# Modulation products of a two-block transformer kernel: from TensorE to VectorE, with their weights outside the ring

## What is computed

```python
sc_x = jax.nn.silu(c)
sc_c = jax.nn.silu(c_ctx)
for l in range(DEPTH):
    mx = (sc_x @ ada_w[l] + ada_b[l]).reshape(bsz, 6, 1, d)
    mc = (sc_c @ ada_w[l] + ada_b[l]).reshape(6, d)
    hx = modulate(rmsnorm_2(x, norm_g[l, 0]), mx[:, 0], mx[:, 1])
```

## Time and profile before

| | |
|---|---|
| median of 3 runs | 4306.5 us (4297.13 to 4309.94) |
| the profiled execution: its own time, its span | 4302.7 us, 4300.9 us |
| mean granted clock of TensorE | 0.955 of full |
| TensorE (PE) matmuls, busy | 3941.1 us, 92% |
| TensorE weight loads (PEld) | 3224.4 us, 75% |
| VectorE (DVE) | 1837.2 us, 43% |
| ScalarE (ACT) | 1383.9 us, 32% |
| GpSimd (POOL) | 1422.2 us, 33% |

### The profile page before, as it was taken

One profiled execution on the slowest core, in us unless ns is written; L12 is line 12 of the kernel. 1 busy time (PEld: TensorE's weight loads), 2 busy tenths in 40 slices (PEclk: granted clock), 3 DMA queues, 4 the chain that ended last, 5 costly groups with the idle time before them and its releaser, 6 DMA issues. The chain is left out here.

```text
span 4300.9 us, 48720 instructions
## 1 busy us (share of the span) xinstructions
PE 3941.1 (92%) x19562; PEld 3224.4 (75%) x19562; DVE 1837.2 (43%) x3076; ACT 1383.9 (32%) x2082; POOL 1422.2 (33%) x644
## 2 busy tenths in 40 slices
PE   6999998999989999899997888899999879999998
PEld 4777766777777776777765777789999668876886
DVE  4544445644554444374354556331111555543113
ACT  3223334332332333432233444231111334443222
POOL 1225543655422453355550110122222100023442
PEclk9999999999999999999998998899999889999999
DMA  2123332444321233234431000112221100012332
GB/s 86 56 61 103 110 91 66 127 127 129 103 61 57 88 116 92 75 118 132 127 109 34 25 25 20 40 44 59 64 64 56 51 15 15 14 50 69 94 97 74
DMA packets 544397, 316.69 MB, mean 74 GB/s; under 512 B 35828, under 2 KB 517167, under 8 KB 544175
## 3 DMA queue, kind: packets, MB, share of 16 engines
q1 hardware_dynamic: 543903, 312.53, 24.6%
q10 hardware_dynamic: 272, 1.05, 0.1%
HBM read 311.44 MB, written 2.10 MB: 73 GB/s over the span
## 5 line engine op out<-in xcount | busy, mean ns | idle before, releaser
L443 POOL TENSOR_TENSOR wlo<-wraw,whi 128x1024 fp32r<-128x1024 f32 (+5 forms) x640 | 1422.0, 2228 | 2843.6 <-ACT whi L436 2842.3
L459 PE MATMUL acc<-hh,whi 128*128 128x512 f32 (+2 forms) x2744 | 1071.7, 391 | 71.0 <-POOL wlo L443 32.8
L461 PE MATMUL acc<-hh,wlo 128*128 128x512 f32 (+2 forms) x2744 | 1040.0, 379 | 0.0
L460 PE MATMUL acc<-hl,whi 128*128 128x512 f32 (+2 forms) x2744 | 1038.2, 378 | 0.0
L436 ACT ACTIVATE whi<-wraw 128x1024 fp32r<-128x1024 f32 (+5 forms) x640 | 625.9, 980 | 866.2 <-DMA wraw<-in_ffn_w 263.4
L459 PEld LDWEIGHTS acc<-hh,whi 128*128 128x128 f32 x2744 | 522.4, 190 | 212.7 <-POOL wlo L443 54.8
L460 PEld LDWEIGHTS acc<-hl,whi 128*128 128x128 f32 x2744 | 523.0, 191 | 91.0 <-issue 11.8
L461 PEld LDWEIGHTS acc<-hh,wlo 128*128 128x128 f32 x2744 | 522.1, 190 | 85.8
L1358 DVE TENSOR_TENSOR t<-acc,sq 128x768 f32<-128x768 f32 (+1 forms) x44 | 36.3, 825 | 501.6 <-PE acc L461 501.6
L459 PE MATMUL ob<-hh,whi 128*128 128x512 f32 (+2 forms) x576 | 219.9, 382 | 20.6 <-DVEq L764 20.1
L660 DVE TENSOR_SCALAR y<-acc 128x512 f32<-128x512 f32 (+1 forms) x80 | 59.6, 745 | 356.4 <-PE acc L461 356.4
(11 more groups left out here) (367 smaller groups left out, 6043.4 us busy)
## 6 DMA issues: line engine op xcount, KB each, us to landing
wraw<-in_ffn_w SPq DMA_DIRECT2D x120, 512.0 KB, 3.7
wraw<-in_w_in SPq DMA_DIRECT2D x102, 512.0 KB, 3.7
wraw<-in_ada_w SPq DMA_DIRECT2D x96, 512.0 KB, 3.9
wraw<-in_w_up SPq DMA_DIRECT2D x88, 512.0 KB, 3.9
wraw<-in_w_down SPq DMA_DIRECT2D x32, 512.0 KB, 4.3
wraw<-in_w_out SPq DMA_DIRECT2D x16, 512.0 KB, 4.1
wraw<-in_w_mkv SPq DMA_DIRECT2D x16, 512.0 KB, 4.0
wraw<-in_ab_w_in SPq DMA_DIRECT2D x14, 512.0 KB, 3.7
```

Source lines behind the costliest of these rows:

```text
L443: e.tensor_tensor(wlo[0:rows, s, a:b, 0:w], wraw[0:rows, s, a:b, 0:w], whi[0:rows, s, a:b, 0:w].bitcast(F32), ALU.subtract).then_inc(lo_re ...
L459: e.matmul(o, wh, xh, start=first, stop=False)
L460: e.matmul(o, wh, xl, start=False, stop=False)
L461: return e.matmul(o, wl, xh, start=False, stop=last)
```

## The change

The modulation slabs leave the ring. A buffer `ada_w` of its own takes one slab (2 x 512 numbers in each of 128 partitions), in the place where `row_f` was, and SyncE loads it straight behind a slab of the ring, when VectorE has used the one before (`ada_used`). ScalarE, GpSimd and TensorE do nothing with it. VectorE multiplies each of its two rows of tiles by the condition of that row, a number per partition, and adds to two running sums (128 x 512 for each of the two conditions), `ada_s` and columns 512 to 767 of `sq`. In the gates it does so behind its reads of gates 0 and 2, in the FFN's up part behind the convolution, between the reads of a pair, in the down part behind a read. The sum over the partitions is left to `pe_ada_out`, now eight f32 matmuls with 128 rows of weights and one column of ones, run behind the first slab of a pair or behind gate 0.

```diff
-        row_f = nc.alloc_sbuf_tensor_at("row_f", [4, AW2], F32, offset=229344 - 4 * AW2)
+        ada_w = nc.alloc_sbuf_tensor_at("ada_w", [P, 2, AW2], F32, offset=229344 - 4 * 3 * AW2)
+        ada_s = nc.alloc_sbuf_tensor_at("ada_s", [P, AW2], F32, offset=229344 - 4 * AW2)
...
         def load(e, c, parts, width=P, cols=None):
...
+            if ada_due and ada_due[0] == n:
+                ada_due.pop(0)
+                load_ada(e, c)
+
+        def load_ada(e, c):
+            n = c.count("ada")
+            l, u, part = n // (4 * ADA), n // 4 % ADA, n % 4
+            w = A["ada_w_2"][bass.ds(l, 1), part * 256:part * 256 + 256, bass.ds(u * AW2, AW2)]
+            if n % (4 * ADA) == 0:
+                e.wait_ge(bi_ready, 4 * l + 4)
+            if n:
+                e.wait_ge(ada_used, n)
+            e.dma_start(ada_w[:, :, :], w.rearrange("o (k p) m -> p (o k) m", p=P)).then_inc(ada_landed, 16)
...
-        def sp_ada(e, c):
...
-            load_wide(e, w.rearrange("o (k p) m -> p (o k) m", p=P))
+        def sp_ada():
+            ada_due.append(len(slabs) + 1)
+
+        ADA_SUMS = [ada_s[:, :].rearrange("p (b a) -> p b a", b=2), sq[:, :, SEQ:TC]]

         def pe_ada(e, c):
             n = c.count("ada")
             if n % 4 == 0 and n // 4 % ADA not in ADA_FLUSH:
                 pe_ada_out(e, c)
-            w = weights(e, c)
-            for j in range(2):
-                k = n % 4 * 2 + j
-                for rows in (whi, wlo):
-                    mm = e.matmul(ob[1][0:4, :], sc4[:, k, :], rows[:, w, 4 * j:4 * j + 4, :].rearrange("p a m -> p (a m)"),
-                                  start=k == 0 and rows is whi, stop=k == KT - 1 and rows is wlo)
-            mm.then_inc(slab_done, 1)
...
+        def pe_ada_out(e, c):
+            n = c.count("ada_out")
+            e.wait_ge(ada_row, c.next(ada_row))
+            if n:
+                e.wait_ge(ada_kept, c.next(ada_kept))
+            for j in range(4):
+                for v, sums in enumerate(ADA_SUMS):
+                    mm = e.matmul(ob[0][:, 2 * j + v:2 * j + v + 1], sums[:, j // 2, j % 2 * P:j % 2 * P + P], edge[:, 4, 0:1],
+                                  start=True, stop=True)
+            mm.then_inc(ada_out, 1)
...
         def dve_ada(e, c):
...
+            e.wait_ge(ada_landed, c.next(ada_landed, 16))
+            if n % 4 == 0 and n:
+                e.wait_ge(ada_out, n // 4)
+            for j in range(2):
+                k = n % 4 * 2 + j
+                w = ada_w[:, j, :].rearrange("p (b a) -> p b a", b=2)
+                if k:
+                    e.wait_ge(ada_sum, c.next(ada_sum, 2))
+                for v, sums in enumerate(ADA_SUMS):
+                    col = scT[:, k, v:v + 1]
+                    if k == 0:
+                        ins = e.tensor_scalar(sums, w, col, None, ALU.mult)
+                    else:
+                        ins = e.scalar_tensor_tensor(out=sums, in0=w, scalar=col, in1=sums, op0=ALU.mult, op1=ALU.add)
+                    ins.then_inc(ada_sum, 1)
+            e.wait_ge(ada_sum, c.at(ada_sum, 2))
+            e.sem_inc(ada_used, 1)
             if n % 4 == 3:
+                c.next(ada_sum, 2)
+                e.sem_inc(ada_row, 1)
...
@@ pe_ffn
-                        if units and j % 2:
+                        if units and j % 2 == 0:
                             pe_ada(e, c)
@@ dve_ffn
                             e.wait_ge(conv_ready, c.next(conv_ready))
+                            dve_ada(e, c)
                             dve_scaled(e, c, zf[:, j, PAD:], s1)
@@ sp_ffn
                         load(e, c, [(0, P, rows_of(up, l, 0, KT, u))])
+                        if ada:
+                            sp_ada()
                         load(e, c, [(0, P, rows_of(up, l, 0, KT, u + FF))])
-                        if ada:
-                            sp_ada(e, c)
@@ gates, on TensorE and VectorE
-                        if br == 1:
+                        if br != 1:
                             pe_ada(e, c)
...
-                    pe_ada(e, c)
```

More of the change, by code:

```diff
@@ L390, in p3 @@
             return ps[0:M, 0:b, 0:n]
-        slabs = []
-        slabs = []
+        slabs, ada_due = [], []
         def load(e, c, parts, width=P, cols=None):
@@ L632, in pe_linear_y, with act_linear_y @@
             turns(e, c, KT // 2, body)
-        def act_linear_y(e, c, ada=(), flush=False, T=None, y=None):
+        def act_linear_y(e, c, T=None, y=None):
             if y is not None:
@@ L1226, in pe_ada, with dve_ada @@
+        def dve_ada(e, c):
+            n = c.count("ada")
+            if n % 4 == 2 and n // 4 % ADA not in ADA_FLUSH:
+                dve_ada_out(e, c)
+            e.wait_ge(ada_landed, c.next(ada_landed, 16))
+            if n % 4 == 0 and n:
+                e.wait_ge(ada_out, n // 4)
             for j in range(2):
                 k = n % 4 * 2 + j
-                for rows in (whi, wlo):
-                    mm = e.matmul(ob[1][0:4, :], sc4[:, k, :], rows[:, w, 4 * j:4 * j + 4, :].rearrange("p a m -> p (a m)"),
-                                  start=k == 0 and rows is whi, stop=k == KT - 1 and rows is wlo)
@@ L1231, in pe_ada @@
-            mm.then_inc(slab_done, 1)
[L1232 to L1254, removed]
-            if n % 4 == 3:
[L1256 to L1264, removed]
@@ L1266, in dve_ada @@
-        def dve_ada(e, c):
-            n = c.count("ada")
-            c.next(slab_done)
-            if n % 4 == 2 and n // 4 % ADA not in ADA_FLUSH:
-                dve_ada_out(e, c)
+                w = ada_w[:, j, :].rearrange("p (b a) -> p b a", b=2)
[8 more added lines that the diff above has]
+                    ins.then_inc(ada_sum, 1)
@@ L1322, in act_ffn @@
                     c.next(act_ready, FT if conv else 2)
-                act_linear_y(e, c, ada_down(p) if conv else (), conv and p == 2, T, y if p == len(FF_PARTS) - 1 else None)
+                act_linear_y(e, c, T, y if p == len(FF_PARTS) - 1 else None)
         def dve_ffn(e, c, T, y, ah, al, conv, l=None):
@@ L1889, in _ @@
             act.sem_inc(cond_ready, 1)
-            act.activation(sc4[:, :, 0:2], scT[:, :, :], ACT.Copy).then_inc(sc_hi, 1)
             act.activation(rope_s[:, :], red[:, :], ACT.Sin).then_inc(act_step, 1)
```

36 lines of the change are left out of this document (5 added, 31 removed).

## The result

The changed kernel takes 4273.68 us (median; 4270.51 to 4276.99) against 4305.37 for the kernel before on the same chip: a ratio of 0.9932, 95% interval 0.9918 to 0.9946. That is 31.7 us less, where 60 were forecast. The profiled execution took 4276.99 us, its span is 4275.2.

A forecast was written before the change was run, and what follows sets the result against it. TensorE was taken to bound the kernel, with VectorE becoming the bound of the FFN's up part. Savings less longer readings gave -96 us, VectorE's give-back +36, so -60 from 4302.7, and 4246 us as median; range 4200 to 4285.

The forecast's parts named there:

- rival of full holds: FFN up part: every split holds VectorE 2.16 us, a pair takes 12.8, +58 given back, 4268 us; chance 0.20.
- Product matmuls, -89.6: Gates and FFNs: 96 modulation slabs leave TensorE at 0.93 us each, 29.9 us in gates, 59.7 in FFNs.
- Waits in the gates, -28: Gates, both layers: TensorE's waits for the sums' row (-14 us) and for GpSimd's late splits (-14 of 22) go.
- the clock, -2: Gates: matmul records that grow from 0.40 to 0.63 us behind a wait for a split are spared, -2 us.
- Reading, +23.6: TensorE's reading of sums grows from 8 to 16 records at 0.12 us, for 24 groups +23.6 us.
- The sum of these, -96: Whole kernel: removed matmuls, removed waits, clock and longer readings together give -96 us, before VectorE's give-back.
- VectorE keeps up: FFN up part: one of two splits falls in idle time, a pair costs about 10.7 us, 4210 us; chance 0.27.
- VectorE's new work: Each slab adds four VectorE operations, 2.8 us on average; an FFN up pair goes from 5.7 to 8.5 us unblocked.
- The give-back, +36: FFN up parts: VectorE needs 270.6 us a layer against TensorE's 252.7, so 18 a layer is lost, +36 us.
- VectorE's 12.3 us a pair: FFN up part: 8.5 us of operations plus two split holds of 1.9 each, over TensorE's 11.2; chance 0.40.
- The tied queue: FFN: SyncE's loads wait on VectorE's last product, VectorE waits 1.3 us a pair, 14.1 a pair, 4325 us; chance 0.08.

The follow-up runs named there:

- e1_no_ffn: The changed kernel without the FFN's modulation work (its slab loads, products and readings of sums): 4154.99 us, ratio 0.9655 to the kernel before.
- e11_psum_all: The changed kernel with the running sums in PSUM in the gates as well as in the FFN: 4191.22 us, ratio 0.9729 to the kernel before.
- e3_psum: The changed kernel with the FFN's running sums in PSUM, only the last of eight products writing SBUF: 4190.57 us, ratio 0.9741 to the kernel before.
- c_after: The changed kernel measured once more, nothing altered: 4268.94 us, ratio 0.9924 to the kernel before.
- e5_late_read: The changed kernel with two sets of sums in the FFN, read by TensorE one slab later: 4268.95 us, ratio 0.9909 to the kernel before.
- e4_two_buf: The changed kernel with a second buffer and semaphore for the FFN's odd slabs of ada_w: 4244.17 us, ratio 0.9847 to the kernel before.
- e6_at_end: The changed kernel with an FFN pair's products moved behind the pair's last operation: 4393.05 us, ratio 1.0199 to the kernel before.
- a1_gap: The changed kernel with an unused 128-byte tile where sc4 had stood, restoring the old addresses behind it: 4285.52 us, ratio 0.9946 to the kernel before.

## Why the prediction was right and wrong

The direction and the range were right; the gain was half of what I forecast, and the time, 4273.7, is nearest to that of the rival of full holds, 4268. By its steps:
- **Product matmuls, -89.6**: right. The floor e1_no_ffn has a layer's FFN at 363.7 instead of 401.9, 38.2 less; 32 slabs of 0.93 and the 7.8 of eight old readings are 37.6.
- **Waits in the gates, -28, and the clock, -2**: right. With the matmuls (-29.8) and the readings (+7.8) my terms make -52 for the two gates stages; they fell by 31 and 24, 55. The granted clock rose from 0.98 to 1.00. VectorE is busy 139 us of 192 there, less than I had, and cost nothing (e11_psum_all).
- **Reading, +23.6**: right to a few us. I took 0.12 us a record, 1.96 for 16; the trace has 1.70. The extra on 24 groups is then 17 us. What I left out is that the records double to 3.43 us where TensorE had waited.
- **The sum of these, -96**: right. e3_psum shows the kernel in which VectorE keeps up: -114, of which 6 to 17 are addresses, -97 to -108.
- **VectorE's new work**: right. 0.75 us an operation, steps of 0.67 and 0.79, both splits on busy time where a pair has no reading, and VectorE the bound of the up part. Its busy share there is 90%, not over 95%.
- **The give-back, +36: this step failed.** c_after against e3_psum gives 78. I had reckoned it over each part from its first read to its last activation: VectorE 22 x 12.3 = 270.6 us a layer, TensorE 252.7. Over both layers these stretches sum to 504.1 us in e3_psum, so TensorE's need was right. In the changed kernel they sum to 571.5 (570.9 in c_after): 13.0 us a pair, and 67 us given back.
  - What was wrong is VectorE's 12.3 us a pair. A pair without a reading takes 12.9, the rival's 12.8: both splits are held nearly whole, 4.2 us together. I had taken 1.9 us a hold between 0.95 and 2.16, on the ground that a split would now and then fall on a PSUM read. It can't where both splits arrive inside four products in a row, and my own text had put them there. The Trainium skill, "SBUF — State Buffer", Who interferes with whom, says the two engines exclude each other for a whole instruction; the trace agrees, to 2.2 of GpSimd's 2.4 us. I had cited it and gone under it.
  - Over all pairs a hold does average 1.9 us (166.4 us for 88 splits), but by luck. Around a reading a pair takes up to 14.9 us, and there VectorE idles, so that one of its splits is held less. This idle time was in no term; the six up parts have 28.9 us of it, 6.4 for ada_w and most of the rest in these waits for TensorE, each within 15 us behind a reading of sums (us, times, longest):

```profile
DVE zf L571 <- PE acc L463: 21.0, 13, 3.0
```

  - Without the waits at readings (e5_late_read) the stretches sum to 562.0, 58 more than in e3_psum: that is the full holds' +58. The waits add some 9 to it.
- **The rest, 10 to 12 us,** was in no term. From a part's last activation to the next part's first read, or the layer's last down read, the changed kernel takes 268.0 us in sum (266.5 in c_after), e3_psum 256.3. I had let TensorE lose at a part's end only what VectorE is late. But behind such a wait (they take 1.9 to 8.6 us in the changed kernel's profile) it can run at the lower of its clock levels for a while, as at 825.54. By the granted clock of the profile that costs 10.0 us in these stretches, and nothing in e3_psum.
- **The tied queue**, a rival at 0.08, isn't what bounds the changed kernel: VectorE waited 10.8 us in all for ada_w. But it sets where the splits fall, 25 to 33 us (e4_two_buf), and with the products some 2.9 us further back it bounds the pair and makes the change a loss (e6_at_end). I priced it only as a late load, not as what brings both splits together.
- **Addresses**: in no term. With the old addresses the change is worth 0.9946, 23 us (a1_gap).

## What to carry to other kernels

Work moved to VectorE beside GpSimd operations should be costed with every GpSimd operation as a full hold where VectorE has no idle time, and placed, or given a PSUM operand, so that the two don't meet: here the place of two running sums was worth 78 us, more than twice the whole change. The longer of two engines' chains is only a lower bound for a stage in which each waits for the other now and then, as at the readings here. A wait moved onto a queue is to be followed to the transfers behind it and to where their work then lands. And before a per-cent difference is explained by a mechanism, compare a stretch that the change left alone: a removed tile shifts every tile behind it.

## What was unexpected of the hardware

- A gapless matmul stream of 384 columns runs at 1134 or 1156 matmuls in 200 us, depending on 128 bytes in the address of the tile it reads; both rates are at a granted clock of 1.00, so the clock doesn't tell them apart.
- A product with a PSUM operand costs VectorE what one with two SBUF operands does (0.75 us), and GpSimd held none of them: the 96 in e3_psum that accumulate in ob take 754 to 757 ns, the 96 in pt 747 to 752, where one with two SBUF operands took up to 2.93 us in the changed kernel's FFN.
- GpSimd is slowed as well: two splits back to back take 4.9 to 5.6 us beside held operations in the changed kernel's first up part, 4.8 to 5.2 in e3_psum's.
- After a wait of 4.83 us TensorE stayed at half clock for 8.6 us, after one of 6.6 us (825.54) for about 3.
